# Seven block products for eight in the down projections of two MLPs

## The reference

```python
def squared_relu_mlp(h, w_up, w_down):      # w_up (1024, 4096), w_down (4096, 1024)
    a = jax.nn.relu(h @ w_up)
    return (a * a) @ w_down

# in each layer:
h2 = rmsnorm(x, p['norm_mlp_g'][i])
x = x + squared_relu_mlp(h2, p['mlp_w_up'][i], p['mlp_w_down'][i])
```

## Time and profile before

| | |
|---|---|
| median of three runs | 1663.29 us |
| profiled execution: span (no other time is given for it) | 1663.9 us |
| mean granted clock of TensorE | 0.976 |
| TensorE matmuls busy | 1560.4 us, 12617 records |
| VectorE busy | 942.6 us |
| ScalarE busy | 593.2 us |
| GpSimd busy | 389.1 us |
| first MLP, by the chain | 595.7 to 971.6 us |
| second MLP, by the chain | 1270.2 to 1648.1 us |

### The profile page before, as it was taken

One profiled execution on the slowest core, in us unless ns is written; L12 is line 12 of the kernel. 1 busy time (PEld: TensorE's weight loads), 2 busy tenths in 40 slices (PEclk: granted clock), 3 DMA queues, 4 the chain that ended last, 5 costly groups with the idle time before them and its releaser, 6 DMA issues.

```text
span 1663.9 us, 30150 instructions
## 1 busy us (share of the span) xinstructions
PE 1560.4 (94%) x12617; PEld 1538.8 (92%) x12617; DVE 942.6 (57%) x1101; ACT 593.2 (36%) x755; POOL 389.1 (23%) x437
## 2 busy tenths in 40 slices
PE   5898988899887999999999999999999999999996
PEld 5888888899887899999999999999999999999996
DVE  4688898863988774343435453464445435344353
ACT  3746644625465342221212343432234212122221
POOL 3076676631777420000000122100001000000001
PEclk9999999899998999999999999999999999999998
DMA  5445354433444323233232333222232332323221
GB/s 162 110 138 155 122 159 144 133 125 112 132 151 131 118 77 102 76 102 98 79 101 77 102 102 102 77 79 77 80 99 77 102 100 79 103 77 102 77 77 52
DMA packets 158919, 173.34 MB, mean 104 GB/s; under 512 B 13912, under 2 KB 146896, under 8 KB 158784
## 3 DMA queue, kind: packets, MB, share of 16 engines
q1 hardware_dynamic: 137032, 131.30, 25.8%
q0 software_dynamic: 9472, 26.50, 4.9%
q10 hardware_dynamic: 12288, 13.71, 2.9%
HBM read 159.53 MB, written 12.21 MB: 103 GB/s over the span
## 4 chain that ended last, share of the span: by engine, by line
PE 64%; DVE 1%; ACT 1%; issue 0%; POOL 0%; ACTq 0%; DVEq 0%
PE ps L500 61%; PE ps L842 1%; PE ps L520 0%; PE ps L810 0%; ACT w_hi L897 0%; PE ps L757 0%; DVE h_lo L1509 0%; PE ps L543 0%; DVE xT L1805 0%; DVE w_lo L1492 0%; POOL ssum L1356 0%; ACT arena L1300 0%; PE ps L834 0%; POOL arena L1424 0%; DVE work L1498 0%
## 5 line engine op out<-in xcount | busy, mean ns | idle before, releaser
L500 PE MATMUL ps<-h_hi,w_hi 128*128 128x260 f32 (+2 forms) x2320 | 485.5, 291 | 12.2 <-issue 4.9
L500 PE MATMUL ps<-h_lo,w_hi 128*128 128x260 f32 (+2 forms) x2320 | 474.9, 287 | 0.1
L500 PE MATMUL ps<-h_hi,w_lo 128*128 128x260 f32 (+2 forms) x2320 | 474.8, 287 | 0.0
L1492 DVE TENSOR_TENSOR w_lo<-w,w_hi 128x2048 fp32r<-128x2048 f32 (+2 forms) x122 | 278.7, 2285 | 185.6 <-ACT w_hi L897 185.6
L500 PEld LDWEIGHTS ps<-h_hi,w_hi 128*128 128x128 f32 x2320 | 368.6, 193 | 14.7 <-issue 12.4
L500 PEld LDWEIGHTS ps<-h_lo,w_hi 128*128 128x128 f32 x2320 | 366.4, 193 | 0.4 <-issue 0.4
L500 PEld LDWEIGHTS ps<-h_hi,w_lo 128*128 128x128 f32 x2320 | 365.9, 192 | 0.0
L897 ACT ACTIVATE w_hi<-w 128x2048 fp32r<-128x2048 f32 (+2 forms) x122 | 229.7, 1884 | 313.2 <-PE ps L500 313.2
L500 PE MATMUL ps<-a_hi,w_hi 128*128 128x260 f32 x1504 | 305.5, 284 | 7.9 <-DVE a_lo L1599 5.5
L500 PE MATMUL ps<-a_hi,w_lo 128*128 128x260 f32 x1504 | 304.4, 284 | 0.0
L500 PE MATMUL ps<-a_lo,w_hi 128*128 128x260 f32 x1504 | 304.1, 284 | 0.0
(11 more groups left out here) (196 smaller groups left out, 1354.0 us busy)
## 6 DMA issues: line engine op xcount, KB each, us to landing
w<-in_mlp_w_up SPq DMA_DIRECT2D x32, 1024.0 KB, 5.7
w<-in_mlp_w_down SPq DMA_DIRECT2D x32, 1024.0 KB, 5.2
w<-in_ssd_w_in SPq DMA_DIRECT2D x16, 1024.0 KB, 6.5
w<-in_cm_w_in SPq DMA_DIRECT2D x16, 1024.0 KB, 5.7
w<-in_ssd_w_in SPq DMA_DIRECT2D x16, 512.0 KB, 5.6
arena<-in_state_ssm POOLq DMA_DIRECT2D x64, 128.0 KB, 3.4
arena<-scr_a ACTq DMA_DIRECT2D x16, 512.0 KB, 3.7
arena<-scr_bc POOLq DMA_DIRECT2D x32, 256.0 KB, 3.7
```

What stands on the lines that cost most here:

```text
L500: mm = pe.matmul(ps[:, 2 * slot + b, 0:tn], w[:, pair.slot, k, col:col + P], x[:, k, t0:t0 + tn], start=(k == 0 and n == 0), stop=(k == ti ...
L1492: nc.vector.tensor_tensor(w_lo[:, pair.slot, k, w], w32[:, pair.slot, k, w], w_hi[:, pair.slot, k, w].bitcast(F32), ALU.subtract).then_inc ...
```

## The change

In chunks 0, 1 and 2 of both MLPs the down projection is done by a scheme of seven block products for eight (Winograd's form of Strassen's). For one down pair the blocks are two output tiles by two halves of the contraction (512 each) by two halves of the tokens (260 each). Weight blocks A11, A12, A22 are taken as they are, and four sums S1 to S4 of blocks are formed on GpSimd (`weight_sums`) from the fp32 weights; on the other side stand the activations' blocks and four differences T1 to T4 (`differences`, GpSimd, from the squared activations). Each product is split into high part and remainder as before and takes 12 matmuls of 260 columns into one bank of its own. Products that several outputs share are kept in `kept` (VectorE, summed over the chunks) and added into `xT` once, on GpSimd (`merge`), before the last chunk's down projection; the others are added to `xT` at once. The last chunk is done plainly, with 48 matmuls per unit.

`w_hi` and `w_lo` become a ring of eight blocks of 512 elements: an up pair or a plain pair has four, a pair of seven products has seven, and a block is split as soon as the block eight places before it has been used. The first up pair of the next chunk is moved ahead of the down pairs. The loops of the MLPs are written out on every engine. Up pairs use all eight banks in turn, and the activations of an up pair have two buffers (`work`, `up_more`). The new tiles lie in the arena, so the engines wait for its former users (`arena_free`) when an MLP begins. The diff's core:

```diff
+class MlpPair(Pair):
+    def __init__(self, J, place, up, c, i, block0, hi0, ups, fast, downs):
+        ...
+        self.seven = not up and not self.plain          # plain: c == CHUNKS - 1
+        self.block0, self.blocks = block0, 7 if self.seven else 4
+        self.bank = 4 if up and (i in (0, 2)) and place else 0
+def mlp_pairs(J, hi0, ups, fast, downs):
+    order = []
+    for c in range(CHUNKS):
+        order += [(True, c, i) for i in range(1 if c else 0, 4)]
+        if c + 1 < CHUNKS:
+            order.append((True, c + 1, 0))
+        order += [(False, c, i) for i in range(4)]
+    ...
+A11, S2, S1, S3, A12, S4, A22 = range(7)
 # SP
-                with sp.Fori(0, CHUNKS) as c:
-                    ...
+                for p in MLP0 if J == J_MLP0 else MLP1:
+                    stage(p, w_block(up, 0, p.c * D + 256 * p.i) if p.up else w_block(down, p.c * D, 256 * p.i))
 # TensorE
+            def seven_products(p):
+                ...
+                if p.i == 0:
+                    pe.wait_ge(b_hi_done, 3 * (4 * (p.c + 1) + (12 if p.J == J_MLP1 else 0)))
+                    pe.wait_ge(b_lo_done, 3 * (4 * (p.c + 1) + (12 if p.J == J_MLP1 else 0)))
+                for n, hi, lo in plan:
+                    (waits: the block's high part and remainder; for even n the reader of the banks)
+                    b = (p.ring + n) % 8
+                    for k in range(4):
+                        for i, (w, act) in enumerate(((w_hi, hi), (w_hi, lo), (w_lo, hi))):
+                            mm = pe.matmul(ps[:, n, 0:TH], blocks(w)[:, b, k, :], act[:, k, :],
+                                           start=(k == 0 and i == 0), stop=(k == 3 and i == 2))
+                    mm.then_inc(unit_done if n > 4 else product_done, 1)
-                with pe.Fori(1, CHUNKS - 1) as c:
-                    chunk(c, False)
 # ScalarE
+            def act_blocks(pairs, first, end):
+                for b in range(first, min(end, BLOCKS)):
+                    p, n = block_of(pairs, b)
+                    if n == 0:
+                        act_e.wait_ge(w_landed[p.slot], p.use(1) * 16)
+                    if p.seven and n in SUMS:
+                        act_e.wait_ge(summed, 4 * p.downs + SUMS[n] + 1)
+                    wait_used(act_e, block_used(pairs, b - 8))
+                    ...
+                    nc.scalar.activation(blocks(w_hi)[:, (p.ring + n) % 8], src, ACT.Copy)\
+                      .then_inc(w_hi_done if n == p.blocks - 1 else block_hi, 1)
+            def up_high(p):
+                ...
+                act_e.wait_ge(up_done, 2 * p.fast + 2)
+                nc.scalar.activation(b_hi[:, 0, p.i, :], src[:, 0, 0:TH], ACT.Copy).then_inc(b_hi_done, 1)
+                nc.scalar.activation(b_hi[:, 1:3, p.i, :], halves(src[:, 1, :]), ACT.Copy).then_inc(b_hi_done, 1)
+                act_e.wait_ge(diff_done, 4 * p.fast + 4)
+                nc.scalar.activation(quarters(a_hi)[:, :, p.i, :], diffs(), ACT.Copy).then_inc(b_hi_done, 1)
 # GpSimd
+            def weight_sums(p):
+                pool.wait_ge(w_landed[p.slot], p.use(1) * 16)
+                ...
+                (four adds of 128x512, each behind the release of its buffer by the down pair before:)
+                (S1 = a21 + a22; S2 = S1 - a11; S3 = a11 - a21; S4 = a12 - S2)
+            def differences(p):
+                ...
+                (four subtractions of 128x260, the first behind the first half of the up pair, the others behind the second)
+            def merge(p):
+                ...
+                (five adds: two of 128x260, three of 128x520 elements)
+            def mlp(pairs):
+                arena_free(pool, pairs)
+                for p in pairs:
+                    if p.place + 2 < len(pairs) and pairs[p.place + 2].seven:
+                        weight_sums(pairs[p.place + 2])
+                    if p.up and not p.plain:
+                        differences(p)
+                for p in pairs:
+                    if p.seven and p.c == CHUNKS - 2:
+                        merge(p)
+            mlp(MLP0)
             add_squares(2)
+            pool.wait_ge(unit_done, MLP0[-1].unit(1, 1))
 # VectorE
+            def up_low(p):
+                ...
+                (remainders: 260 elements into b_lo, 520 into b_lo, 1040 into a_lo, each behind its b_hi_done)
+            def keep_products(p, n, first):
+                dst, src = kept_of(p, first, 2), ps[:, n - 1:n + 1, 0:TH]
+                ...
+                nc.vector.tensor_tensor(dst, src, dst, ALU.add).then_inc(added, 1)
+            def add_products(p, half):
+                ...
+                dst = xT[:, 2 * p.i + 1, 0:TH] if half else halves(xT[:, 2 * p.i, :])
+                src = ps[:, A22, 0:TH] if half else ps[:, A12:S4 + 1, 0:TH]
+                nc.vector.tensor_tensor(dst, src, dst, ALU.add).then_inc(evac_done, 1)
+            # the list of VectorE (prepare: split the blocks up to this one); ScalarE's has the same order
+                for p in pairs:
+                    b = p.block0
+                    if p.place == 0:
+                        prepare(8)
+                        inv_rms(n)
+                        arena_free(dve, pairs)
+                    if waiting and (p.up or p.c == CHUNKS - 1 and p.i == 0):
+                        if p.up:
+                            prepare(b + 8)
+                        up_low(waiting)
+                        waiting = None
+                    prepare(b + 8)
+                    if p.up:
+                        waiting = p
+                        up_tile(p, 0)
+                        prepare(b + 10)
+                        up_tile(p, 1)
+                    elif p.seven:
+                        prepare(b + 9)
+                        keep_products(p, S2, 0)
+                        prepare(b + 11)
+                        keep_products(p, S3, 2)
+                        prepare(b + 13)
+                        add_products(p, 0)
+                        prepare(b + 14)
+                        add_products(p, 1)
+                    else:
+                        (plain pairs: wait for merged, then as before)
```

More of the change, by code:

```diff
@@ new lines, in mlp_pairs @@
+def mlp_pairs(J, hi0, ups, fast, downs):
[5 more added lines that the diff above has]
+        order += [(False, c, i) for i in range(4)]
+    pairs, block = [], 0
+    read = {1: ("evac", Pair(J - 1).unit(0, 1)), 0: ("evac", Pair(J - 1).unit(1, 1)), 2: None, 3: None}
+    if J == J_MLP0:
+        read = {1: ("evac", Pair(J - 1).unit(0, KT - 1)), 0: ("evac", Pair(J - 1).unit(0, KT)), 2: None, 3: None}
+    for place, (up, c, i) in enumerate(order):
+        p = MlpPair(J, place, up, c, i, block, hi0, ups, fast, downs)
+        pairs.append(p)
+        for region, after in p.regions():
+            p.free[region] = read[region]
+            read[region] = after
+        block += p.blocks
+        hi0 += p.blocks - 1
+        ups += up
+        fast += up and not p.plain
+        downs += p.seven
+    return pairs
@@ new lines, with block_of, block_used @@
+MLP0 = mlp_pairs(J_MLP0, 0, 0, 0, 0)
+MLP1 = mlp_pairs(J_MLP1, MLP0[-1].hi0 + 3, 16, 12, 12)
+SEVENS = [p for p in MLP0 + MLP1 if p.seven]
+BLOCKS = MLP0[-1].block0 + 4
+A11, S2, S1, S3, A12, S4, A22 = range(7)
+SUMS = {S1: 0, S2: 1, S3: 2, S4: 3}
+def block_of(pairs, b):
+    p = [p for p in pairs if p.block0 <= b][-1]
+    return p, b - p.block0
+def block_used(pairs, b):
+    if b < 0:
+        return "unit", Pair(pairs[0].J + b // 4).multiplied()
+    p, n = block_of(pairs, b)
+    return p.used(n)
@@ L760, in out_tr @@
                   .then_inc(ty_done, 1)
-            def mlp(n, J):
[L764 to L783, removed]
-                with pe.Fori(1, CHUNKS - 1) as c:
-                    chunk(c, False)
-                chunk(CHUNKS - 1, False, final=True)
@@ new lines, in mlp_unit @@
+            def mlp_unit(p, half, hi, lo, k_ready):
+                n = 2 * half + 1
+                if half:
+                    pe.wait_ge(w_hi_done, p.times(1, 1))
+                    pe.wait_ge(w_lo_done, p.times(1, 1))
+                else:
+                    pe.wait_ge(block_hi, p.hi0 + n + 1)
+                    pe.wait_ge(block_lo, p.hi0 + n + 1)
+                bank = p.bank + 2 * (1 - half)
+                wait_read(pe, p.free[bank // 2])
+                for k in range(KT):
+                    if k_ready:
+                        k_ready(k)
+                    b = (p.ring + 2 * half + k // 4) % 8
+                    for i, (w, x) in enumerate(((w_hi, hi), (w_hi, lo), (w_lo, hi))):
+                        for t, (t0, tn) in enumerate(EVEN):
+                            mm = pe.matmul(ps[:, bank + t, 0:tn], blocks(w)[:, b, k % 4, :], x[:, k, t0:t0 + tn],
+                                           start=(k == 0 and i == 0), stop=(k == KT - 1 and i == 2))
+                mm.then_inc(unit_done, 1)
@@ L896, in split_w @@
                 k = slice(0, pair.tiles())
[L897 removed]
```

(4 more changed lines are left out.)

363 lines of the change are left out of this document (300 added, 63 removed).

## The result

The changed kernel takes 1627.92 us (median of four runs, 1626.29 to 1630.82), the kernel before 1663.78 (four runs on the same chip, 1662.7 to 1668.78): ratio 0.9776 [0.9755, 0.9797], 36 us faster. The forecast was 1626.0. The profiled execution took 1630.82 us; its span is 1629.1, at a mean granted clock of 0.969.

What follows compares the result with a forecast made beforehand. The prediction took TensorE's matmuls to bound both MLPs. From the span, 1663.9 - 34.6 (matmuls) - 4.8 (loops) + 2.0 (late down pairs) = 1626.5, stated as 1626 us; range 1617 to 1641.

Steps and rivals of the forecast that it cites:

- Matmuls removed: Down pairs of both MLPs: 288 fewer matmuls at 120.1 ns, 34.6 us off, all on the path.
- pace of a product: Down pairs' products: matmuls keep 120.1 ns despite fresh weights each and twelve adding into one bank.
- upper bound of 0.13: Products' matmuls at 0.13 us each instead of 0.1201: 20 us more, 1646 as a rival, chance 0.08.
- The loops go: Second MLP, third chunk's start: written-out code removes TensorE's fetch hole and the slower clock behind it, 4.8 us off.
- fetch hole: Rival: TensorE's idling for instruction fetch stays or moves into the longer written-out code, 1630.8 us; chance 0.12.
- D0 late: First down pair of each chunk with products starts 0.3 us late, 2 us in all; bounds 0 and 8.4.
- list of 24.5 us: VectorE and GpSimd work ahead of a chunk's first down pair, one after the other, against 23.1 us available.
- port lock in full: Rival: VectorE and GpSimd strictly take turns, first down pair 1.4 us late in six chunks, 1632.3 us; chance 0.14.
- Other waits: Waits for the arena and the first MLP's end cost 0; 1.3 us per MLP if cover were gone.
- VectorE and GpSimd fit: VectorE alone needs 7.3 of 10.1 us per down pair, 7.9 of 11.5 per up pair; GpSimd 32.6 of 86.5 per chunk.
- slower rival: GpSimd's adds run as slowly as in the scan stage, 8.7 us late per chunk, 1676 us; chance 0.06.
- likeliest case: The forecast itself, 1626 us, with its own range 1619 to 1630; chance 0.60.

Runs made afterwards that it cites:

- the written-out kernel before: The kernel before with only TensorE's loop over the two middle chunks of each MLP written out: 1661.05 us, ratio 0.9986 to the kernel before.
- the version with blocks first: The changed kernel with ScalarE copying the second up pair's weight blocks ahead of the norm's root at each MLP's start: 1625.61 us, ratio 0.977 to the kernel before.

## Why the prediction was right, and where it wasn't

*Matmuls removed, pace of a product* (-34.6): right. 288 fewer, 119.9 ns each in the products; the upper bound of 0.13 had no part. One bank for twelve matmuls and a new weight tile for each cost nothing that the trace shows.

*The loops go* (-4.8): right in the cause, by the written-out kernel before. In the trace it is 4.8 and 4.2 us; timed alone 2.3 [0.5, 4.3], so 4.8 was probably too much for the mean execution. No fetch hole came up elsewhere: in the version with blocks first TensorE's run through each MLP is unbroken. The instruction queue bears out the prediction's reading that one of the two returns fetched and the other did not.

*D0 late* (+2.0): wrong, nothing was late. Each D0 had 2.8 us to spare. The list of 24.5 us was off in two places. It left out the two evacuations of U3 (0.69 each). And the two sums for D1 don't stand ahead of D0 on GpSimd: they stand behind U3's differences and begin at 650.26, when those are done, so they can only slow the last remainder. Of the 24.5 us about 0.7 came later (half of the second sum for D1, which ran until 654.3); the other 23.8, GpSimd's durations alone being estimates, were done in the 20.0 us from 633.1 to 653.1, 84% of one after the other (79% with the two evacuations), where I had taken 92% from one pair of rows. The rival of the port lock in full falls with it: the Trainium skill (SBUF — State Buffer, SBUF: two separate sides) has the two engines' shared port held for a whole instruction, one of them blocked fully; by it alone the list takes its full length but for the evacuation, which has one input in SBUF: 23.1 us, where it took 20.0. The rows agree on which operations are touched (two inputs in SBUF: 1.04 us instead of 0.68; one from PSUM: 0.69 still), and not on the amount.

*Other waits* (0): this is the term that failed, by 4.5 us. I costed VectorE's and ScalarE's waits at the start of an MLP at nothing, and named a split of 1.3 us per MLP as the price if the cover were gone; it was 2.3. The diff's core shows VectorE's side, four blocks ahead of its reciprocal, and says that ScalarE's list has the same order. At the start of an MLP it hasn't: there ScalarE's blocks stand behind its square root, which waits for TensorE. I read the order within VectorE and took ScalarE's to be the same. In the kernel before the split was done at 600.7 to 603.0 and the reciprocal began at 603.3:

```profile
600.74 2.29 DVE L1492 TENSOR_TENSOR w_lo<-w,w_hi 128x2048 fp32r<-128x2048 f32 x1 [1.34 <-ACT w_hi L897]
603.29 3.40 DVE L1515 RECIPROCAL rstd<-ssum 128x520 f32<-128x520 f32 x1 [0.26 <-ACT ssum L929]
```

After the change ScalarE's root comes first, VectorE's blocks begin at 603.1 and the reciprocal at 605.5:

```profile
601.84 0.70 ACT L1137 ACTIVATE ssum<-ps,eps 128x520 f32<-128x520 f32 x1 [4.11 <-PE ps L705]
603.08 2.50 DVE L2131 TENSOR_TENSOR w_lo<-w,w_hi 128x512 fp32r<-128x512 f32 x4 [3.82 <-ACT w_hi L1434]
```


*VectorE and GpSimd fit*: right as a whole, with durations that were too short: 1.04 instead of 0.68 for a block, 1.6 to 1.9 instead of 1.29 for a sum, 0.8 to 1.2 instead of 0.75 for a difference. They stretched in each other's time, not in TensorE's. The slower rival (GpSimd as slow as in the scan stage) was near in durations and still wrong, as it added them up as if the two engines had run one after the other.

Together 1626.5 - 2.0 + 4.6 = 1629.1, the span of the profiled execution: two errors of opposite sign, so that the forecast came as near as it did by some luck, and a median inside the likeliest case's own range.

## What to carry to other kernels

- Where TensorE sets the time, a matmul saved is worth its pace, and the question is what the saving asks of the others: find the shortest stretch between a result and the first matmul that needs it, and list what stands ahead of it on each engine. Here one up pair moved into that stretch was worth 74 us (1703 against 1629).
- Read the start of a stage on every engine, each list by itself: a wait that two lines in the other order would hide is easily costed at nothing, and cost 4.5 us here.
- Durations of VectorE and GpSimd operations that slow each other (1.04 us instead of 0.68 here) can't be added up, nor can one taken alone be used: take the time that a list of both took together.

## What the runs showed of the hardware that was not expected

- A loop's return cost 2.4 and 2.7 us of idle TensorE, and with the clock 4.2 and 4.8, in the second MLP of the kernel before in both profiles; the same loop's return in the first MLP cost nothing in either. In the first MLP the instruction queue moved six packets in the loop's first turn and none at the return and in the second turn; in the second MLP it moved three around the return and seven in the turn behind it. Why the one was fetched again and the other not stays open.
- VectorE and GpSimd, both busy nearly all the time, finished a list of operations with inputs in SBUF in 84% of the sum of its durations alone (GpSimd's are estimates from adds of 256 and 520 elements), while a block or a sum is recorded 1.3 to 1.5 times as long as alone.
- Some idle stretches of TensorE cost more than themselves: behind 9 us of idling the first products step by 0.22 us instead of 0.12 for about 3 us (granted clock 0.82 from 650 to 660 us). Others don't: behind the 2.3 us at the first MLP's start the changed kernel kept a granted clock of 1.00 (602 to 622 us), and the 384 matmuls took 46.34 us where others took 46.14.
